# A two-block transformer kernel on one core: two-head attention steps, a shorter lag between gathered rows, and query weights loaded earlier

## What is computed

```python
qp = (xb @ wq).reshape(PEER_TOKEN_BLOCK, PEER_HEADS, 2, PEER_DKEY // 2)
s = jnp.einsum('thcd,hcnd->thcn', qp, subkeys)
...                                   # top 16 of each half, top 16 of the 256 sums: eidx, sc
gates = jax.nn.softmax(sc, axis=-1)
ue = u[eidx]; ve = v[eidx]
act = jax.nn.gelu(jnp.einsum('td,thkd->thk', xb, ue), approximate=False)
return jnp.einsum('thk,thkd->td', (gates * act), ve)
```

## Time and profile before

| | us |
|---|---|
| median of three executions | 1515.4 |
| the profiled execution | 1518.93 |
| its span, first to last instruction | 1517.1 |

### The profile page before, as it was taken

One profiled execution on the slowest core, in us unless ns is written; L12 is line 12 of the kernel. 1 busy time (PEld: TensorE's weight loads), 2 busy tenths in 40 slices (PEclk: granted clock), 3 DMA queues, 4 the chain that ended last, 5 costly groups with the idle time before them and its releaser, 6 DMA issues.

```text
span 1517.1 us, 20596 instructions
## 1 busy us (share of the span) xinstructions
PE 1364.3 (90%) x7648; PEld 1026.5 (68%) x7648; DVE 1025.8 (68%) x1830; ACT 503.1 (33%) x848; POOL 587.3 (39%) x630
## 2 busy tenths in 40 slices
PE   8899898788877777877798899999999989999998
PEld 7788896244422222322243499999999986899998
DVE  5997799958575767777544577777876376544454
ACT  2222213121111212221212274544335676444442
POOL 1420174777777777777777200122220002000000
PEclk9999999999989999999999999999999998999999
DMA  9866598999999999999999757688973430345540
GB/s 384 313 234 234 222 419 336 419 420 413 418 421 419 419 420 419 420 420 420 419 419 420 293 215 274 221 320 313 320 270 125 167 136 32 125 167 190 183 166 28
DMA packets 114078, 454.16 MB, mean 299 GB/s; under 512 B 12048, under 2 KB 29600, under 8 KB 100816
## 3 DMA queue, kind: packets, MB, share of 16 engines
q0 software_dynamic: 81616, 297.84, 48.9%
q1 hardware_dynamic: 32384, 155.31, 27.9%
HBM read 452.06 MB, written 1.05 MB: 299 GB/s over the span
## 4 chain that ended last, share of the span: by engine, by line
PE 49%; DMA 20%; DVE 11%; POOL 10%; issue 7%; ACT 1%; SPq 1%; DVEq 0%; POOLq 0%; ACTq 0%
PE psum L2265 16%; POOL arena L543 10%; DMA arena<-u_d,arena 10%; PE psum L1875 9%; PE psum L2279 8%; DMA arena<-v_d,arena 7%; DVE arena L1408 4%; PE psum L1818 3%; PE psum L2156 2%; PE psum L1906 2%; DMA arena<-w_ada 1%; PE psum L1933 1%; PE psum L2105 1%; PE psum L2013 1%; PE psum L1815 1%
## 5 line engine op out<-in xcount | busy, mean ns | idle before, releaser
L2156 PE MATMUL psum<-arena 128*128 128x512 f32 x952 | 472.4, 623 | 116.1 <-DMA arena<-v_d,arena 114.1
L1408 DVE CUSTOM_DVE_ANT_0 arena<-arena,psum 128x1024 f32<-128x1024 f32 x256 | 306.6, 1220 | 176.7 <-DMA arena<-u_d,arena 175.9
L2156 PEld LDWEIGHTS psum<-arena 128*128 128x128 f32 x952 | 164.9, 191 | 384.5 <-DMA arena<-v_d,arena 256.6
L543 POOL DMA_INDIRECT arena<-u_d,arena x256 | 241.9, 945 | 128.4 <-issue 50.4
L543 POOL DMA_INDIRECT arena<-v_d,arena x256 | 243.9, 953 | 78.1 <-issue 75.1
L1067 DVE TENSOR_TENSOR wlo<-ring,whi 128x2048 fp32r<-128x2048 f32 x69 | 158.2, 2292 | 86.4 <-ACT whi L611 86.4
L778 ACT ACTIVATE arena<-ident,arena 128x128 f32<-128x128 f32 x238 | 89.5, 397 | 354.3 <-PE psum L2156 318.9
L2265 PE MATMUL psum<-xh,whi 128*128 128x256 f32 x704 | 202.1, 287 | 1.6 <-DVE xl L1061 1.4
L2265 PE MATMUL psum<-xl,whi 128*128 128x256 f32 x704 | 199.2, 283 | 0.0
L2265 PE MATMUL psum<-xh,wlo 128*128 128x256 f32 x704 | 199.1, 283 | 0.0
L611 ACT ACTIVATE whi<-ring 128x2048 fp32r<-128x2048 f32 x69 | 131.3, 1902 | 23.7 <-PE psum L1875 18.9
(11 more groups left out here) (310 smaller groups left out, 2289.9 us busy)
## 6 DMA issues: line engine op xcount, KB each, us to landing
ring<-w_ffn SPq DMA_DIRECT2D x44, 1536.0 KB, 6.8
second<-w_ada POOLq DMA_DIRECT2D x64, 384.0 KB, 5.9
arena<-w_ada SPq DMA_DIRECT2D x50, 384.0 KB, 7.6
ring<-w_inproj SPq DMA_DIRECT2D x14, 1024.0 KB, 8.6
ring<-w_qkv SPq DMA_DIRECT2D x12, 1024.0 KB, 4.9
ring<-w_l0in SPq DMA_DIRECT2D x10, 1024.0 KB, 5.9
ring<-w_peerq SPq DMA_DIRECT2D x6, 1024.0 KB, 8.3
sq<-w_ada SPq DMA_DIRECT2D x14, 384.0 KB, 8.0
```

The source lines that it names most:

```text
L543: g.indirect_dma_start(S["rows"][:, p % GRING, :], None, u_d if kind == "u" else v_d, bass.IndirectOffsetOnAxis(S["idx"][:, n // SLOTS, n ...
L1408: v.tensor_tensor_reduce(row, row, xrow[n // SLOTS], 1.0, 0.0, ALU.mult, ALU.add, S["act"][:, n // SLOTS, n % SLOTS:n % SLOTS + 1]).then_i ...
L2156: ins = t.matmul(vacc[tt][:, at], S["diag"][:, c % DIAGS, :], row[:, at], start=(n % SLOTS == 0), stop=(n == LAST_PE[tt]))
```

## The change

**Loads.** `load_query(j)` holds what stood in the loop. Query unit 0 is now issued after the load of output unit 2 and the modulation pieces behind it, ahead of output unit 3, and waits for `at_s`; unit 1 follows the last modulation piece. Their two places in `arena` are exchanged, and GpSimd waits once, at gather 11, for `query(1, 1)`.

**PEER.** LAG is 22. Gelu and `weights` go by 16 rows (one head) instead of 32; the first `weights` comes at u row 17, between the two `top_rows` of the third batch; the steps of this batch come at rows 13, 18, 20 and 22. Query units 2 to 7 use banks 6 and 7. Units 2 to 5 and one batch of scores stand ahead of the v rows; units 6 and 7 are cut in quarters of eight matmuls between v rows 3 to 24, and the other scores, two groups of transposes and the 48 modulation columns follow between v rows 1 to 91. 9 of the last v rows go to VectorE.

**Attention.** Each step takes two heads (384 columns of each, in two banks, with one ScalarE or VectorE instruction). The masks are gone from VectorE and GpSimd; TensorE adds the mask to the scores with four single-pass matmuls of 128 columns a pair (`eye` times `strict`). The two heads' score matmuls and value matmuls stand beside each other. `first_out` goes in one pair at a time. Behind the first two pairs stand eight matmuls each whose result nobody reads.

```diff
-LAG = 38
+LAG = 22
+BLOCK = 16
-TOP_AT = ((15, 17, 19, 21), (6, 9, 12, 15))
-V_DVE = [n for n in range(221, 256, 2)]
+TOP_AT = ((13, 18, 20, 22), (6, 9, 12, 15))
+V_DVE = [n for n in range(239, 256, 2)]
...
+        def unit_bank(g):
+            return bank[(6 if UNIT0["peerq"] + 2 <= g < UNIT0["l0in"] else 0) + g % 2]
...
 # SyncE
+            def load_query(j):
+                if j == 0:
+                    sp.wait_ge(at_s, 6)
+                elif j == 1:
+                    sp.wait_ge(rec_row, 2)
+                elif j < 6:
+                    sp.wait_ge(unit_done, UNIT0["outproj"] + j - 1)
+                else:
+                    sp.wait_ge(unit_done, UNIT0["peerq"] + j - 3)
+                s = QUERY_AS[j] % RING
+                sp.wait_ge(landed[s], 16 * (QUERY_AS[j] // RING))
+                sp.dma_start(query_weights(j), w_d["peerq"][j]).then_inc(landed[s], 16)
                     if g == 16:
                         load_ada(ADA_LATE + 6)
+                        load_query(0)
             load_ada(ADA_OPS)
+            for j in range(1, UNITS["peerq"]):
+                load_query(j)
...
 # GpSimd
-                if p in (11, 13):
-                    pool.wait_ge(unit_done, UNIT0["peerq"] + (p - 11) // 2 + 1)
+                if p == 11:
+                    pool.wait_ge(unit_done, UNIT0["peerq"] + 2)
-            for h in range(SBH):
-                pool.wait_ge(z_w, h + 1)
-                ...
-                g.tensor_tensor(w, w, m, ALU.mult).then_inc(z_wm, 1)
+            g.tensor_scalar(m, m, -NEG, NEG, ALU.mult, ALU.add).then_inc(z_neg, 1)
...
 # ScalarE, PEER (lam_a's two steps and query units 2 to 7 now stand here)
+            query_out(2)
+            query_out(3)
+            scores_in(2)
             gelu(0)
+            query_out(4)
             for c, n in enumerate(V_PE):
+                if n in (2, 15, 27):
+                    query_out({2: 5, 15: 6, 27: 7}[n])
+                if n == 4:
+                    scores_in(3)
+                if n in (31, 33, 35, 37, 39):
+                    scores_in(4 + (n - 31) // 2)
-                if n % 32 == 29 and n // 32 < 7 or n == 220:
-                    gelu(n // 32 + 1)
+                if n % BLOCK == 13 and n // BLOCK < 15:
+                    gelu(n // BLOCK + 1)
 # ScalarE, attention
+            act.wait_ge(z_neg, 1)
+            a.activation(r32(S["strict"]), S["sbmask"][:, 1, 0:P], ACT.Copy)
+            a.activation(r32(S["eye"]), ident[:, :], ACT.Copy).then_inc(z_mask, 1)
...
+            def z_first(pr):
+                act.wait_ge(z_ps, pr + 1)
+                z = S[f"za{pr % 2}"]
+                seq.mark(a.activation(z, z_bank(pr), ACT.Abs))
+                seq.wait()
+                if pr >= 4:
+                    z_copy(pr - 4)
+                seq.mark(a.activation(z, z, ACT.Exp, scale=-1.0))
+                seq.wait()
+                a.activation(z, z, ACT.Ln, bias=col("one")).then_inc(z_ln, 1)
+            z_first(0)
+            split(UNIT0["l1out"])
+            z_first(1)
+            value_out(3)
+            for i in range(2, SBH // 2):
+                z_first(i)
+                z_second(i - 2)
+                if i == 3:
+                    split(UNIT0["l1out"] + 1)
...
 # VectorE, PEER
-                if gp and k == 1:
-                    weights(gp - 1)
+                if n == 17:
+                    weights(0)
+                if n >= 32 and n % BLOCK == 3:
+                    weights(n // BLOCK - 1)
...
 # VectorE, attention
+            def z_first(pr):
+                z, sp = z_bank(pr), S[f"za{pr % 2}"]
+                dve.wait_ge(z_ln, pr + 1)
+                v.scalar_tensor_tensor(sp, z, 0.0, sp, ALU.max, ALU.add).then_inc(z_sp, 1)
+                dve.wait_ge(z_sp, pr + 1)
+                if pr >= 3:
+                    dve.wait_ge(z_w, pr - 2)
+                v.scalar_tensor_tensor(S[f"zl{pr % 3}"], z, 1.0, sp, ALU.mult, ALU.subtract).then_inc(z_ls, 1)
+            for i in range(SBH // 2 + 1):
+                if i < SBH // 2:
+                    z_first(i)
+                if i == 0:
+                    split(UNIT0["l1out"])
+                if 1 <= i:
+                    z_second(i - 1)
+                if i == 3:
+                    split(UNIT0["l1out"] + 1)
+                if i >= 3:
+                    z_low(i - 3)
...
 # TensorE, PEER
+            for j in range(2, 6):
+                query_start(j)
+                features(UNIT0["peerq"] + j, xn, w=query_weights(j))
+                if j == 3:
+                    scores(2)
...
+                if n == 1:
+                    scores(3)
+                if n % 3 == 0 and 3 <= n <= 24:
+                    query_part(6 + (n // 3 - 1) // 4, (n // 3 - 1) % 4)
+                if n in (28, 30, 32, 34, 36):
+                    scores(4 + (n - 28) // 2)
...
 # TensorE, attention (z_scores(0) ahead of the last qkv unit, z_scores(1) in its middle)
+            def z_scores(pr):
...
+                for c0, q0 in ((0, 0), (P, P)):
+                    for c in range(2):
+                        q, k = (S[n][64 * c:64 * c + 64, pr, :] for n in ("qT", "kT"))
+                        t.matmul(at[c][:, 2 * c0:2 * c0 + T - q0], k[:, c0:c0 + P], q[:, q0:T], start=(c0 == 0), stop=False,
+                                 skip_group_check=True)
+                for c in range(2):
+                    for c0 in (0, T):
+                        ins = t.matmul(at[c][:, c0:c0 + P], r32(S["eye"]), r32(S["strict"]), start=False, stop=True,
+                                       skip_group_check=True)
+            for pr in range(SBH // 2):
+                z_after(pr)
+                if pr + 2 < SBH // 2:
+                    z_scores(pr + 2)
+                if pr < 2:
+                    for i in range(8):
+                        t.matmul(bank[0][:, 0:T], r32(xh[:, i, 0:P]), r32(xh[:, i, :]), start=True, stop=True,
+                                 skip_group_check=True)
+                if pr >= 2:
+                    z_value(pr - 2)
+                if pr >= 4:
+                    first_out((pr - 4,))
+            first_out((4,))
+            z_value(6)
+            first_out((5,))
+            z_value(7)
             first_out((6, 7))
```

More of the change, by code:

```diff
@@ L746, in _, with query_out @@
             query_in(1, 1)
-            for j in range(2, 8):
+            def query_out(j):
                 read_unit(UNIT0["peerq"] + j, ACT.Copy, flat(S["qpT"][:, 2 * j:2 * j + 2, :]))
[L749 to L757, removed]
             def gate_exp(gp):
@@ L1035, in _ @@
+            z_second(6)
+            z_copy(4)
+            z_second(7)
+            for i in range(5, SBH // 2):
+                z_copy(i)
             into_ffn(1, 5, H_L1, mcol[:, 72:80])
@@ L1753, in z_low, with z_second @@
+            def z_second(pr):
+                dve.wait_ge(z_af, pr + 1)
+                dve.wait_ge(z_ls, pr + 1)
+                to = S[f"zl{pr % 3}"]
+                v.tensor_tensor(to, to, z_sum, ALU.subtract).then_inc(z_arg, 1)
             def z_low(pr):
                 dve.wait_ge(z_out, pr + 1)
[L1756 to L1766 removed]
+                v.tensor_tensor(r32(S["oTl"][:, pr, :]), z_mix(pr), S["oTh"][:, pr, :], ALU.subtract).then_inc(z_lo, 1)
@@ L1770, in _ @@
+            z_low(7)
             gated_residual("l1out", 64, 1)
@@ L1901, in split_rows @@
                 for tt in range(TT):
+                    if between is not None and tt:
+                        between()
                     for k in range(KT):
@@ L2353, in z_value, with z_after @@
-            def z_value(h):
-                pe.wait_ge(z_wm, h + 1)
-                pr = h // 2
-                if h % 2 == 0 and pr >= 2:
-                    pe.wait_ge(z_lo, pr - 1)
-                o = bank[6 + pr % 2][64 * (h % 2):64 * (h % 2) + 64, :]
-                w = S[f"wz{h % 2}"]
-                t.matmul(o[:, 0:T], S["vrow"][:, 0, h * HD:(h + 1) * HD], w[:, 0:T], start=True, stop=False,
-                         skip_group_check=True)
-                t.matmul(o[:, P:T], S["vrow"][:, 1, h * HD:(h + 1) * HD], w[:, T:T + P], start=False, stop=True,
-                         skip_group_check=True).then_inc(z_o, 1)
+            def z_after(pr):
+                pe.wait_ge(z_sp, pr + 1)
+                if pr:
+                    pe.wait_ge(z_arg, pr)
+                for c in range(2):
+                    o, lk = bank[6 + c], S[f"za{pr % 2}"][:, c, :]
+                    t.matmul(o[:, 0:T], S["tri"], lk[:, 0:T], start=True, stop=False, skip_group_check=True)
+                    t.matmul(o[:, P:T], ones[:, :], lk[:, T:T + P], start=False, stop=True, skip_group_check=True)
+                    ins = t.matmul(o[:, T:T + P], S["tri"], lk[:, T:T + P], start=True, stop=True,
+                                   skip_group_check=True)
+                ins.then_inc(z_af, 1)
@@ new lines, in z_value @@
+            def z_value(pr):
+                pe.wait_ge(z_w, pr + 1)
+                if pr == 0:
```

(11 more changed lines are left out.)

246 lines of the change are left out of this document (89 added, 157 removed).

## The result

| | us |
|---|---|
| kernel before, median of four executions | 1516.36 (1512.99 to 1519.77) |
| changed kernel, median of four executions | 1490.23 (1489.09 to 1490.58) |
| ratio, 95% interval | 0.9832 [0.9811, 0.9854] |
| profiled execution and its span | 1489.97, 1488.1 |

Forecast were a median of 1487 (1477 to 1502) and a profiled execution of 1490.4. Faster by 1.7%, which is well outside 0.3%.

A forecast was written before the change was run, and what follows sets the result against it. Full DMA engines were taken to bound the gather stage, a three-engine chain with TensorE's list longest the attention. 11.9+16.5, rounded to 28.5 us, took the profiled 1518.93 to 1490.4, less 3.5 gave a median of 1487, range 1477 to 1502.

The forecast's parts named there:

- Start: First query product: TensorE's 4.03 us wait and half clock go, 5.8 us earlier; query unit 1 no wait, bounds 0 and 2.6.
- Gather 40: Gather stage: gather 40 leaves at 241.9 instead of 253.77 us, once u row 23 is used; 11.9 us gained.
- the term: Gather stage (PEER): 11.9 us gained by earlier start and smaller index-wait hole; limits 3.3 and 13.0 us.
- of which 3.3 are the earlier start: Gather stage: 3.3 of the 11.9 us come from gather 11 leaving at 197.2 instead of 200.5.
- Costed at nothing: Gather stage: query quarters between v rows, 16-row weights and five final v rows cost nothing, the last at most 1 us.
- Attention: Stick-breaking attention: two heads share the array, 2.5 us of waits, 16.8 us gained, 16.5 after ScalarE's copies; limits 3.3 and 20.
- Drain: Attention masks: changing tiling mode drains TensorE, 0.09 us each, 0.7 in all, left out of prices; sum 27.8 instead of 28.5.
- The two terms: Gather stage 11.9 us and attention 16.5 us, together 28.4, with rounding 28.5.
- The median: Whole kernel: 1487 us, from a profiled execution of 1490.4 less the old median's 3.5 us offset.

The follow-up runs named there:

- idx_early: Changed kernel with only GpSimd's wait for the third index set put back to gather 32, where the old lag had it; 1498.9 us, 0.9883 of before.
- q0_late: Changed kernel with query unit 0 loaded behind the last output unit and the modulation pieces again; 1495.8 us, 0.9862 of before.
- peer_only: Changed kernel with all attention edits taken back, keeping the new loads and lag; 1502.7 us, 0.9911 of before.
- wide_mask: Changed kernel with each head's two 128-column mask matmuls made one of 256 columns; 1488.4 us, 0.9803 of before.
- no_unread: Changed kernel without the unread matmuls in the first two attention pairs; 1490.0 us, 0.9814 of before.
- best: Changed kernel with wide_mask's edit, mask-operand copies moved into the qkv loop, and output unit 1's split two pairs later; 1489.3 us, 0.9809 of before.
- lag18: Changed kernel with v rows 18 instead of 22 behind the u rows; 1490.6 us, 0.9827 of before.
- lag14: Changed kernel with v rows 14 instead of 22 behind the u rows; 1614.9 us, 1.0645 of before.

## Why the prediction was right

**Start.** Taking the 2.14 us off, the second 128 tokens' product starts 5.9 us earlier (5.8 forecast), the first gather 3.1 (3.1), gather 11 at 197.1 on the old scale (197.2). No half clock, no wait for query unit 1.

**Gather 40** comes at 242.2 on the old scale; 241.9 was forecast, and 12.2 us at the last gather stand against 11.9. VectorE's list in the changed kernel, at its start and at its end (u row 13, the first step of the third batch, u row 23):

```profile
210.44 1.22 DVE L1436 CUSTOM_DVE_ANT_0 arena<-arena,psum 128x1024 f32<-128x1024 f32 x1 [0.99 <-DMA arena<-u_d,arena]
...
211.59 0.48 DVE L1349 MAX8 arena<-arena 128x8 f32<-128x128 f32 x2
...
238.58 1.21 DVE L1436 CUSTOM_DVE_ANT_0 arena<-arena,psum 128x1024 f32<-128x1024 f32 x1
```

Row 23 begins at 240.7 on the old scale and ends at 241.9 (240.7 and 241.8 forecast). (GpSimd's row names TensorE ahead of gather 40, as the last to signal; but of v rows that gather needs only the first two, which were done before 230. What ended last of what it needs is row 23.) At the start of the list a part of the hit is luck. The prediction has the batch begin when its scores are read, at 213.5; it began at 213.7, but the scores had been read 0.5 us before, and what came last was the data of u row 13, for which VectorE had waited. The prediction does not have that wait.

What the term had wrong is in its words "of which 3.3 are the earlier start". With the early start but the old wait (idx_early) 3.0 us of the 12.2 are left, with the later wait but the old start (q0_late) 4.2. Most of the gain needs both, because both act on when gather 40 can leave (8.7 and 7.6 us later without the one and the other).

**Costed at nothing.** Query units between v rows, weights by 16 rows and the five v rows at the end: the engines run at 417 GB/s throughout, and the first scores of the attention come 11.7 us earlier than before, counted as above, in peer_only, wide_mask and no_unread. In the changed kernel's own profiled execution they come 10.4 us earlier: behind the last v row TensorE falls to half clock for a moment.

```profile
848.28 3.51 PE L2221 MATMUL psum<-sq,arena 128*128 128x128 f32 x16 [0.85 <-ACT sq L810]
```

The same 16 records took 2.05 us before, 1.5 less. It shows in q0_late too and not in the other profiles of lag 22; what decides it stays open.

**Attention.** 16.2 us shorter against 16.8 forecast, 50.34 against 49.7. The chain of the changed kernel, from the first pair to the fifth, and its end:

```profile
1217.45 0.85 PE psum L2379 x8
1218.30 0.59 PE psum L2383 x4
...
1239.12 2.20 DVE wlo L1099
...
1243.53 0.95 DVE second L1779
...
1244.62 0.67 PE psum L2406 x2
...
1245.74 0.43 PE psum L2406 x2
...
1248.06 0.80 PE psum L2423 x8
1248.86 0.91 PE psum L2437 x6
...
1267.79 11.52 PE psum L1903 x96
```

Scores 0.85 and values 0.80 came as priced: the array is shared. Masks cost 0.59 a pair, not 0.44; the output part 0.91, not 0.72. The sums cost 1.75 in this chain, not 2.14; counted from start to start, as in the earlier trace rows, a pair's take 1.85 (1230.22 to 1232.07). In the earlier trace rows half-size work stands on both sides of a head's sums, and the next matmul starts 0.53 us behind the first of them and 0.32 behind the last; behind full-array work the first takes 0.44 (1230.22 to 1230.66), and between a pair's two heads the shape does not change. The prediction had read that price, 0.09 us a change, and yet taken it into a pair's sums four times, where it is due once or twice. The errors of the prices nearly cancel: TensorE's list is 47.0 us long, 47.2 by the prediction's prices. And what TensorE waits for:

```profile
PE psum L2406 <- DVE second L1779: 2.4, 3, 1.1
```

2.4 us in three waits against 2.5, the largest 1.1 at the fifth pair against 1.4 (of the remaining 0.9 us, 0.7 are the first records behind these waits, 0.67 us each in the chain instead of 0.43). Place and size were right, the cause given was not: the split (L1099) stands in the chain there, but best shows that the wait stays without it.

Behind the two copies on ScalarE the eleventh qkv unit waits 0.3 us, as taken.

**Drain.** By the rule of the Trainium skill (TensorEngine Tiling (Array Packing), Key Properties) and the row's 0.09 us the sum was 27.8 instead of 28.5. The two terms as measured, 12.2 and 16.2 less 0.3 for the copies, make 28.1 and cannot decide between them. The 0.19 us of wide_mask that are not columns speak for the rule, and so do the sums, where it works the other way: they have fewer changes of shape than their price held.

**The median** is 1490.23, 3.2 us above the 1487 forecast. Of this 1.0 is the old kernel's own median (1515.4 by three executions, 1516.4 by four), and the rest is the gain, 26.1 us instead of 28.5. The step that failed is the size of the sum, then, and the profiled execution met its forecast (1489.97, 1490.4 forecast) in part by luck: between the two spans lie 29.0 us, of which 2.14 are the start that wanders, 10.35 the stretch from there to the attention, 16.15 the attention and 0.36 the rest. The change's own part is the middle two, some 26.5 us, much as by the medians. Against 28.5 some 1.5 us went to the half clock behind the last v row, and 0.6 are missing in the attention. The 3.5 us between the old kernel's profiled execution and its median, which the prediction took over, were no property of a program either: the changed kernel's profiled execution lies 0.3 us below its median. The old kernel's executions spread over 1512 to 1521 us in these runs, with the mean granted clock (on one chip 0.992 at 1512.5 and 0.985 at 1520.7), those of the changed one over 1489.1 to 1490.6, all four at 0.995.

## What to carry to other kernels

Where a stage is bound by its transfers, price an edit by the transfer time it restores, and count the slow refill behind a hole as well as the dry stretch. A list that is late all the time cost next to nothing here as long as the ring held (lag18); find the number of places between the row that needs and the row that gives, because beyond it the cost was a cliff (lag14). Two edits that act on the same wait are not to be priced one by one. Measure from a point that both kernels share, and take neither the difference of two profiled executions for the gain nor that between one such execution and a median for a property of the program.

## What was not expected of the hardware

The two halves of the array overtook each other, so that the order of two heads' half-size matmuls was free (0.85 and 0.86 us for a pair's scores in the two orders). After a dry stretch the 16 DMA engines came back at 298 GB/s for 6 us though gathers were issued every 1.24 us. The granted clock fell to 0.94 over the whole gather stage of lag18 with 1.3 us lost at most, while the DMA engines moved 417 GB/s as before. And TensorE kept the full clock in the attention at 7.58 of 10 us busy.
